# Matmuls of an identity matrix into an unread PSUM bank, in thirteen places where TensorE waits, in a hybrid decoder trunk

## The chip, the core and the metric

The kernel runs on one core of a Trainium2 chip. The metric is the device time of one execution in microseconds (us); lower is better. "TensorE" is the matmul engine, "VectorE", "ScalarE" and "GpSimd" are the elementwise engines; in the rows of the profile they are PE (PEld for its weight loads), DVE, ACT and POOL. SP is the engine that issues the weight transfers.

## What is computed

Two layers on 256 tokens of width 1024 in float32, batch 1:

```python
# layer 0
h = h + retention_mixer(rmsnorm(h), w_in, w_out)          # 4 heads, chunks of 128
h = h + swiglu(rmsnorm(h), w_gu, w_down)                  # 1024 -> 2 x 3584 -> 1024
# layer 1
h = h + conv_module(rmsnorm(h), w_pw1, w_dw, ln, w_pw2)   # depthwise width 31, LayerNorm
h = h + moe_swiglu(rmsnorm(h), w_router, w_gu, w_down)    # top 2 of 8 experts of 3584
return rmsnorm(h)
```

## The kernel before

The 256 tokens are two tiles of 128 rows. All weights stream from HBM in blocks of 1 MB (128x2048 floats): SP loads a block into one of six `raw` buffers, ScalarE copies it to `whi` (line 407, rounded to the fp32r type of TensorE), VectorE subtracts to get the rest `wlo` (line 702), and TensorE makes each product as three fp32r matmuls of 128x512 (lines 1142, 1143, 1146: high by high, high by low, low by high). Experts with at most 64 tokens use two matmuls for three (lines 1149, 1150). `whi` and `wlo` have three buffers each. Semaphores written out by hand order everything; each engine runs its own program in order, so an instruction that stands behind a waiting one waits too.

Between the weight stages TensorE has little to do and waits for the other engines:

- A norm (`turn(k)`, line 1231). ScalarE sums squares, GpSimd takes the root, VectorE writes the normalised `z` in quarters, TensorE transposes each quarter (128x128, float32) against `ident`, and ScalarE and VectorE evacuate the result to `xh` and `xl` (`xx` in the rows, lines 413 and 726). `turn(0)` opens the kernel, `turn(1)` precedes the dense SwiGLU, `turn(2)` the convolution, `turn(3)` the router.
- The LayerNorm of the convolution: sums over channels with a matrix of ones (lines 1421 and 1425), the scale spread over partitions (line 1429), and then the matmuls of `w_pw2`, which wait for `xl`.
- The router: logits (line 1443, 8 columns each), ranks (lines 1448 to 1452), the gather of the first expert's tokens with a one-hot matrix (lines 1459 and 1460, 128 columns), then `gates_first`, the first expert's gate columns.
- The end: `scatter_before(NE)` puts the last expert's output back (lines 1476 and 1477) after ScalarE and VectorE have split it.

`ident` is the first 128 columns of the constant `mats`, a transfer that ScalarE's queue issues first (line 391). A float32 matmul shows as two records in the trace, a float32 transpose and an fp32r matmul as one.

Of the kernel before, what the change touches and what calls it, by code (L numbers as in the profile page):

```python
# [17 lines left out]
SEQ, D, P = 256, 1024, 128  # L18
# [25 lines left out]
def trunk(nc, x, positions, norm_mix_g, norm_ffn_g, final_norm_g, ret_w_in, ret_w_out, conv_w_pw1,  # L44
# [6 lines left out]
    with ctx:  # L51
# [24 lines left out]
        ident, earlier, ones, iota, fold = (mats[:, i, :] for i in range(5))  # L76
# [74 lines left out]
        bank = [ctx.enter_context(nc.psum_tensor(f"bank{i}", [P, BANK], f32)) for i in range(8)]  # L151
# [109 lines left out]
        def need_before(eng, e):  # L261
            return eng.value_load(plan[0:1, 0, bass.ds(e, 1)], min_val=0, max_val=3)
# [877 lines left out]
        def _(pe):  # L1140
# [85 lines left out]
            def turn(k):  # L1226
                for t in range(TILES):
                    for c in range(DC):
                        if c % 4 == 0:
                            pe.wait_ge(z_done, 4 * k + 2 * t + c // 4 + 1)  # L1230
                        last = nc.tensor.transpose(bank[2 * t + c // 4][:, c % 4 * P:(c % 4 + 1) * P],
                                                   z[:, t, c * P:(c + 1) * P], ident)
                        if c % 4 == 3:
                            last.then_inc(zT_done, 1)

            pe.wait_ge(L["mats"], 16)
            turn(0)
            for n in range(3):
                if n == 2:
                    pe.wait_ge(small_sb, 2)  # L1240
                for half in range(2):
                    columns(2 * n + half, bank[2 * n:2 * n + 2], half, 0 if n == 0 else None)
                if n == 0:

                    pe.wait_ge(L["wdw"], 16)
                    pe.wait_ge(L["small"], 48)
                    for a in range(2):
                        nc.tensor.transpose(bank[4][:, a * 124:(a + 1) * 124], wdw[:, a, :], ident[0:124, 0:124])
                    nc.tensor.transpose(bank[4][:, 256:280], small[:, :], ident[0:24, 0:24]).then_inc(small_ps, 1)
# [6 lines left out]
            for m in range(8):  # L1256
                h = m // 2
                pe.wait_ge(acc_free, (4, 4, 10, 10, 11, 11, 12, 12)[m])
                for cc in range(2):
                    c = 2 * h + cc  # L1260
# [85 lines left out]
            def hT_turn(s):  # L1346
                pe.wait_ge(hid_done, s + 1)
                chunk_turn(0, FULL)
                chunk_turn(1, FULL).then_inc(hT_ps, 1)
# [12 lines left out]
            def step(base, s, first=False, six=0):  # L1362
# [8 lines left out]
                rows(base + 5, hTh, hTl, 2, False, False, six)  # L1371
                hT_turn(s)

            turn(1)
            pe.wait_ge(xl_done, 6)
            for half in range(2):
# [9 lines left out]
            rows(B_PW1 - 2, hTh, hTl, 0, False, False)  # L1386
            rows(B_PW1 - 1, hTh, hTl, 2, False, True)

            turn(2)
            pe.wait_ge(xl_done, 10)  # L1390

# [8 lines left out]
            for b in range(8):  # L1400
                n = b // 2
# [6 lines left out]
            for m, (c, k) in enumerate(PE_TAPS):  # L1408
                if m == PE_FIRST:
# [4 lines left out]
                                        start=k == VECTOR_TAPS.get(c, 0), stop=k == TAPS - 1)  # L1414
                last.then_inc(tap_done, 1)
            for n, c in enumerate((5, 6, 0, 1, 2, 3, 4, 7)):
                if c >= 5:
                    pe.wait_ge(y_pe, c - 4)
                else:
                    pe.wait_ge(y_done, 1)  # L1420
                last = nc.tensor.matmul(bank[0][:, 0:SEQ], ones, y[:, c, :], start=n == 0, stop=n == DC - 1)
            last.then_inc(mu_ps, 1)
            for c in range(DC):
                pe.wait_ge(sq_done, c + 1)
                last = nc.tensor.matmul(bank[1][:, 0:SEQ], ones, sq[:, c, :], start=c == 0, stop=c == DC - 1)
            last.then_inc(var_ps, 1)
            for t in range(TILES):
                pe.wait_ge(lnd_done, t + 1)
                last = nc.tensor.matmul(bank[2][:, t * P:(t + 1) * P], ones, diag[:, t, :], start=True, stop=True)
            last.then_inc(lnb_ps, 1)  # L1430
            for r in range(4):
                pe.wait_ge(vl_done, 2 * r + 2)
                rows(B_PW2 + r, xh, xl, 2 * r, r == 0, r == 3)

            turn(3)

            pe.wait_ge(res_done, 6)
            pe.wait_ge(L["wr"], 16)
            for t in range(TILES):
                pe.wait_ge(hT32_done, t + 1)  # L1440
                pe.wait_ge(hT32b_done, t + 1)
                for c in range(DC):
                    last = nc.tensor.matmul(bank[4][:, t * NE:(t + 1) * NE], hT32[:, c, t * P:(t + 1) * P], wr[:, c, :],
                                            start=c == 0, stop=c == DC - 1)
            last.then_inc(lg_ps, 1)

            pe.wait_ge(sel_done, 1)
            nc.tensor.matmul(bank[5][:, 0:NE], earlier, rk[:, 4, 0, :], start=True, stop=True)
            nc.tensor.matmul(bank[5][:, NE:2 * NE], earlier, rk[:, 4, 1, :], start=True, stop=False)
# [4 lines left out]
            def gather(e, tile):  # L1454
                for c in range(DC):
                    dst = bank[2 * tile + c // 4][:, c % 4 * P:(c % 4 + 1) * P]
                    for t in range(TILES):
                        where = onehot[:, t, tile * P:(tile + 1) * P]
                        nc.tensor.matmul(dst, zh[:, t, c * P:(c + 1) * P], where, start=t == 0, stop=False)  # L1459
                        last = nc.tensor.matmul(dst, zl[:, t, c * P:(c + 1) * P], where, start=False, stop=t == TILES - 1)  # L1460
                return last
# [18 lines left out]
            def scatter_before(e):  # L1480
                pe.wait_ge(yl_done, e + 1)
                with pe.If(need_before(pe, e) > 1):
                    pe.wait_ge(y2l_done, wide_before(pe, e))
                    scatter(2)
                with pe.Else():
                    scatter(1)
# [12 lines left out]
            def expert(e, kind, need):  # L1499
                six, done, tiles = STEPS * e, STEPS * e + STEPS, 2 if kind == WIDE else 1  # L1500
                gates_end = nothing(bank[0])
                if kind == WIDE:
                    gather(e, 1).then_inc(gather2_ps, 1)
                    scatter_before(e)
                    pe.wait_ge(xel2_done, wide_before(pe, e) + 1)
                    gates_first(1, six).then_inc(pe_done, 2)
                else:
                    gates_end.then_inc(pe_done, 2)
                    scatter_before(e)
                pe.wait_ge(hTl_done, done)  # L1510
                expert_columns(B_MOE + 2, bank[2:4], 0, kind, need, six)
                expert_columns(B_MOE + 3, bank[2:4], 1, kind, need, six)
                pe.wait_ge(res_done, 2 * e + 8)
                onehot_turn(tiles)
                for n in range(2):
                    nc.tensor.matmul(DOWN[0][n][:, :], zeros[:, 0:P], zeros[:, :], start=True, stop=False)
                if kind == WIDE:
                    pe.wait_ge(ohT_done, e + 1)
                    for n in range(2):
                        nc.tensor.matmul(DOWN[1][n][:, :], zeros[:, 0:P], zeros[:, :], start=True, stop=False)  # L1520
                expert_turn(done, kind, need)
                with pe.Fori(0, STEPS - 1) as i:
                    pe.wait_ge(silu_done, done + 1 + i)
                    columns(B_MOE + 4, bank[0:2], 0, tiles=tiles, six=six + i)
                    columns(B_MOE + 5, bank[0:2], 1, tiles=tiles, six=six + i)
                    pe.wait_ge(hTl_done, done + 1 + i)
                    expert_columns(B_MOE + 6, bank[2:4], 0, kind, need, six + i)
                    expert_columns(B_MOE + 7, bank[2:4], 1, kind, need, six + i)
                    expert_rows(B_MOE + 8, 0, False, kind, need, six + i)
                    expert_rows(B_MOE + 9, 2, False, kind, need, six + i)  # L1530
                    expert_turn(done + 1 + i, kind, need)
                pe.wait_ge(silu_done, done + STEPS)
                pe.wait_ge(onehot_done, e + 2)
                gather(e, 0).then_inc(gather_ps, 1)
                pe.wait_ge(hTl_done, done + STEPS)
                expert_rows(B_MOE + 40, 0, False, kind, need, six)
                expert_rows(B_MOE + 41, 2, True, kind, need, six)

            pe.wait_ge(zh_done, 3)
            pe.wait_ge(zl_done, 2)  # L1540
            pe.wait_ge(onehot_done, 1)
            gather(0, 0).then_inc(gather_ps, 1)
            pe.wait_ge(plan_done, 1)
            pe.wait_ge(moe_set, 5)
            with pe.Fori(0, NE) as e:
                need = need_of(pe, e)
                pe.wait_ge(xel_done, e + 1)
                gates_first(0, STEPS * e)
                with pe.If(need < 1):
                    expert(e, HALF_FULL, need)  # L1550
                with pe.Else():
                    with pe.If(need < 2):
                        expert(e, FULL, need)
                    with pe.Else():
                        expert(e, WIDE, need)
            scatter_before(NE)


# [43 lines left out]
```

## Time and profile before

| | us |
|---|---|
| median of 3 runs | 1738.55 (1737.4 to 1740.38) |
| profiled execution | 1737.84 |
| its span, first to last instruction | 1736.0 |
| TensorE busy in the span | 1621.6 (93%) |
| VectorE busy | 1254.5 (72%) |
| ScalarE busy | 1022.7 (59%) |
| mean granted TensorE clock | 0.977 of full speed |

The granted clock is the speed at which TensorE was let run: 1.00 is 2.4 GHz, 0.50 is 1.2 GHz. The ends of matmuls in the trace are modelled: their busy times overlap, and the distance from one start to the next tells the pace.

### The profile page before, as it was taken

Reading aid. Unit: us, or ns where it says so; the run is one execution under the profiler, and the core shown is the slowest. Engines: PE = TensorE matmul, PEld = TensorE weight load, DVE = VectorE, ACT = ScalarE, POOL = GpSimd, SP = SyncE. Lnnn points to the kernel's source line nnn. Section 1 sums busy time; section 2 is a strip of 40 time slices with the busy share of each in tenths; the row PEclk is TensorE's granted clock in tenths of the full one; section 3 lists DMA queues with packets and bytes.
Section 4 is the critical chain, followed back from the end, with each engine's and each line's share of the span. In section 5 each row is a group of like instructions: output and inputs, shape, how many; then the busy total and the mean of one; then the engine's idle time right before and its main releaser. Section 6 shows DMA issues by size and latency. Waiting matters only on the chain.

```text
span 1736.0 us, 20901 instructions
## 1 busy us (share of the span) xinstructions
PE 1621.6 (93%) x7353; PEld 1317.2 (76%) x7354; DVE 1254.5 (72%) x1024; ACT 1022.7 (59%) x872; POOL 120.9 (7%) x91
## 2 busy tenths in 40 slices
PE   7999989999899779989999989989999899999996
PEld 5887878888788667767778878878888777777775
DVE  5745554544569559979988878845555499999996
ACT  4344344334339437878777767744444478788784
POOL 0000000000000003003030030001000030300300
PEclk9999999999999869999999999999999999999998
DMA  9652545555442018999999979946666499999994
GB/s 354 197 194 109 182 150 194 181 189 193 166 174 74 25 43 326 393 351 368 397 366 375 368 284 369 375 145 225 211 199 212 148 354 395 378 391 395 371 395 171
DMA packets 191587, 450.75 MB, mean 260 GB/s; under 512 B 8492, under 2 KB 8892, under 8 KB 191420
## 3 DMA queue, kind: packets, MB, share of 16 engines
q1 hardware_dynamic: 189212, 445.35, 71.3%
q10 hardware_dynamic: 2336, 4.85, 0.8%
q8 instruction: 28, 0.46, 0.1%
q14 instruction: 11, 0.09, 0.0%
HBM read 449.13 MB, written 1.05 MB: 259 GB/s over the span
## 4 chain that ended last, share of the span: by engine, by line
PE 70%; DVE 11%; DMA 9%; ACT 5%; issue 4%; SPq 0%; ACTq 0%; POOL 0%; DVEq 0%; POOLq 0%
PE bank L1142 19%; PE bank L1143 19%; PE bank L1146 19%; DMA raw<-in_moe_w_down 9%; DVE wlo L702 6%; ACT whi L407 4%; PE bank L1149 3%; PE bank L1150 3%; DVE y L940 2%; PE bank L1460 1%; PE bank L1459 1%; PE bank L1341 1%; PE bank L1343 1%; DVE res L1095 1%; ACT sgate L496 1%
## 5 line engine op out<-in xcount | busy, mean ns | idle before, releaser
L702 DVE TENSOR_TENSOR wlo<-raw,whi 128x2048 fp32r<-128x2048 f32 x422 | 963.4, 2291 | 313.7 <-ACT whi L407 312.3
L407 ACT ACTIVATE whi<-raw 128x2048 fp32r<-128x2048 f32 x422 | 805.3, 1915 | 430.8 <-PE bank L1146 320.0
L1142 PE MATMUL bank<-whi,xx 128*128 128x512 f32 x1184 | 473.5, 400 | 29.9 <-DVE xx L1064 8.7
L1143 PE MATMUL bank<-wlo,xx 128*128 128x512 f32 x1184 | 466.7, 394 | 0.0
L1146 PE MATMUL bank<-whi,xx 128*128 128x512 f32 x1184 | 466.1, 394 | 0.0
L1142 PEld LDWEIGHTS bank<-whi,xx 128*128 128x128 f32 x1184 | 226.1, 191 | 80.9 <-issue 19.9
L1146 PEld LDWEIGHTS bank<-whi,xx 128*128 128x128 f32 x1184 | 225.5, 190 | 48.3
L1143 PEld LDWEIGHTS bank<-wlo,xx 128*128 128x128 f32 x1184 | 225.9, 191 | 45.1
L376 POOL TENSOR_SCALAR onehot<-mats,slot 128x64 fp32r<-128x64 f32 x64 | 110.3, 1746 | 906.8 <-PE bank L1466 906.8
L1149 PE MATMUL bank<-whi,hT 128*128 128x512 f32 x336 | 138.8, 413 | 24.0 <-DVE wlo L702 23.7
L1149 PE MATMUL bank<-whi,xx 128*128 128x512 f32 x336 | 134.0, 399 | 2.6 <-DVE wlo L702 2.4
L1150 PE MATMUL bank<-wlo,hT 128*128 128x512 f32 x336 | 132.2, 394 | 0.0
L1150 PE MATMUL bank<-wlo,xx 128*128 128x512 f32 x336 | 131.2, 390 | 0.0
L502 ACT ACTIVATE hT<-bank 128x512 fp32r<-128x512 f32 x77 | 44.6, 598 | 116.2 <-PE bank L1341 60.9
L1142 PE MATMUL bank<-whi,hT 128*128 128x512 f32 x280 | 110.0, 393 | 2.5 <-DVE hT L873 2.5
L1143 PE MATMUL bank<-wlo,hT 128*128 128x512 f32 x280 | 110.2, 393 | 0.0
L1149 PEld LDWEIGHTS bank<-whi,hT 128*128 128x128 f32 x336 | 63.1, 188 | 61.5 <-DVE wlo L702 49.6
L1146 PE MATMUL bank<-whi,hT 128*128 128x512 f32 x280 | 109.0, 389 | 0.0
L873 DVE TENSOR_TENSOR hT<-bank,hT 128x512 fp32r<-128x512 f32 x77 | 51.5, 684 | 41.8 <-ACT hT L502 41.6
L1149 PEld LDWEIGHTS bank<-whi,xx 128*128 128x128 f32 x336 | 63.0, 188 | 24.1 <-DVE wlo L702 11.8
L1150 PEld LDWEIGHTS bank<-wlo,xx 128*128 128x128 f32 x336 | 63.1, 188 | 12.3
L1150 PEld LDWEIGHTS bank<-wlo,hT 128*128 128x128 f32 x336 | 63.2, 188 | 11.6
(203 smaller groups left out, 1280.2 us busy)
## 6 DMA issues: line engine op xcount, KB each, us to landing
raw<-in_moe_w_gu SPq DMA_DIRECT2D x224, 1024.0 KB, 8.0
raw<-in_moe_w_down SPq DMA_DIRECT2D x112, 1024.0 KB, 7.9
raw<-in_ffn_w_gu SPq DMA_DIRECT2D x28, 1024.0 KB, 5.1
raw<-in_ret_w_in SPq DMA_DIRECT2D x24, 1024.0 KB, 5.8
raw<-in_ffn_w_down SPq DMA_DIRECT2D x14, 1024.0 KB, 4.9
raw<-in_conv_w_pw SPq DMA_DIRECT2D x12, 1024.0 KB, 5.1
raw<-in_ret_w_out SPq DMA_DIRECT2D x8, 1024.0 KB, 4.8
res<-in_x SPq DMA_DIRECT2D x2, 512.0 KB, 4.8
```

What stands on the lines that cost most here:

```text
L376: last = nc.gpsimd.tensor_scalar(onehot[:, n // 2, at_:at_ + HALF], iota[:, h * HALF:(h + 1) * HALF], slot[:, e + 1, n, h:h + 1], None, AL ...
L407: nc.scalar.activation(whi[base % SPLIT][:, :], raw[base % RAW][:, :], ACT.Copy).then_inc(hi_done, 1)
L496: last = nc.scalar.activation(sgate[:, t, :], bank[t][:, :], ACT.Silu)
L502: last = nc.scalar.activation(hTh[:, :, t, :], bank[2 + t][:, :].rearrange("p (c n) -> p c n", c=4), ACT.Copy)
L702: nc.vector.tensor_tensor(wlo[base % SPLIT][:, :], raw[base % RAW][:, :], whi[base % SPLIT][:, :].bitcast(f32), ALU.subtract).then_inc(lo_ ...
L873: last = nc.vector.tensor_tensor(hTl[:, :, t, :], bank[2 + t][:, :].rearrange("p (c n) -> p c n", c=4), hTh[:, :, t, :].bitcast(f32), ALU. ...
L940: ins = nc.vector.scalar_tensor_tensor(y[:, c, :], uT[:, c, k:k + SEQ], w, y[:, c, :], ALU.mult, ALU.add)
L1142: nc.tensor.matmul(dst, ah, bh, start=start, stop=False)
L1143: last = nc.tensor.matmul(dst, ah, bl, start=False, stop=stop and al is None)
L1146: return nc.tensor.matmul(dst, al, bh, start=False, stop=stop)
L1149: nc.tensor.matmul(dst, both, bh, start=start, stop=False)
L1150: return nc.tensor.matmul(dst, both, bl, start=False, stop=stop)
```

## The change

A helper `warm` issues n float32 matmuls whose two operands are both `ident`, with 128 columns, each into the same columns of a PSUM bank that nobody reads before it is written again. It is called thirteen times (236 matmuls), each time ahead of a wait. Nothing waits for these matmuls, and nothing but the constants has to be there for them to start.

```diff
+            def warm(dst, n):
+                for _ in range(n):
+                    nc.tensor.matmul(dst[:, 0:P], ident, ident, start=True, stop=True)
+
             pe.wait_ge(L["mats"], 16)
+            warm(bank[7], 24)
             turn(0)
+            warm(bank[7], 20)
             for n in range(3):
...
+            warm(bank[7], 14)
             turn(1)
             pe.wait_ge(xl_done, 6)
...
+            warm(bank[3], 14)
             turn(2)
             pe.wait_ge(xl_done, 10)
...
+                    if c == 0:
+                        warm(bank[2], 18)
                     pe.wait_ge(y_done, 1)
                 last = nc.tensor.matmul(bank[0][:, 0:SEQ], ones, y[:, c, :], start=n == 0, stop=n == DC - 1)
             last.then_inc(mu_ps, 1)
+            warm(bank[3], 10)
             for c in range(DC):
                 pe.wait_ge(sq_done, c + 1)
...
             last.then_inc(var_ps, 1)
+            warm(bank[3], 16)
             for t in range(TILES):
                 pe.wait_ge(lnd_done, t + 1)
...
             last.then_inc(lnb_ps, 1)
+            warm(bank[3], 22)
             for r in range(4):
                 pe.wait_ge(vl_done, 2 * r + 2)
                 rows(B_PW2 + r, xh, xl, 2 * r, r == 0, r == 3)
 
+            warm(bank[3], 14)
             turn(3)
...
             last.then_inc(lg_ps, 1)
 
+            warm(bank[7], 18)
             pe.wait_ge(sel_done, 1)
...
+            warm(bank[7], 26)
             pe.wait_ge(zh_done, 3)
             pe.wait_ge(zl_done, 2)
             pe.wait_ge(onehot_done, 1)
             gather(0, 0).then_inc(gather_ps, 1)
+            warm(bank[7], 18)
             pe.wait_ge(plan_done, 1)
...
+            warm(bank[0], 22)
             scatter_before(NE)
```

TensorE's program at its beginning, of the kernel before (`turn(0)` and the first matmuls on weights), and of the changed kernel:

```order
L1139 UNCONDITIONAL_BRANCH
L1231 MATMUL bank<-mats,z 128x128 x16
L1142 MATMUL bank<-whi_55,xx 128x512
L1143 MATMUL bank<-wlo_58,xx 128x512
L1146 MATMUL bank<-whi_55,xx 128x512
```

```order
L1139 UNCONDITIONAL_BRANCH
L1238 MATMUL bank<-mats 128x128 x24
L1231 MATMUL bank<-mats,z 128x128 x16
L1238 MATMUL bank<-mats 128x128 x20
L1142 MATMUL bank<-whi_55,xx 128x512
L1143 MATMUL bank<-wlo_58,xx 128x512
L1146 MATMUL bank<-whi_55,xx 128x512
```

The transposes now stand behind 24 of the helper's matmuls (L1238), and the first matmul on weights behind 20 more.

TensorE's program around the router, of the kernel before (the logits, the five rank matmuls, and the first two of 32 gather matmuls):

```order
L1231 MATMUL bank<-mats,z 128x128 x16
L1443 MATMUL bank<-wr,hT_108 128x8 x16
L1448 MATMUL bank<-rk,mats 128x8
L1449 MATMUL bank<-rk,mats 128x8
L1450 MATMUL bank<-rk,mats 128x8
L1451 MATMUL bank<-rk,mats 128x8
L1452 MATMUL bank<-rk,mats 128x8
L1459 MATMUL bank<-onehot,zh 128x128
L1460 MATMUL bank<-onehot,zl 128x128
```

The same place in the changed kernel, whose lines stand lower by 4 to 17 (L1238 is the helper's matmul):

```order
L1238 MATMUL bank<-mats 128x128 x14
L1231 MATMUL bank<-mats,z 128x128 x16
L1457 MATMUL bank<-wr,hT_108 128x8 x16
L1238 MATMUL bank<-mats 128x128 x18
L1463 MATMUL bank<-rk,mats 128x8
L1464 MATMUL bank<-rk,mats 128x8
L1465 MATMUL bank<-rk,mats 128x8
L1466 MATMUL bank<-rk,mats 128x8
L1467 MATMUL bank<-rk,mats 128x8
L1238 MATMUL bank<-mats 128x128 x26
L1474 MATMUL bank<-onehot,zh 128x128
L1475 MATMUL bank<-onehot,zl 128x128
```

Three runs of the helper's matmuls stand here between rows that followed each other directly before: 14 ahead of the transposes, 18 between logits and ranks, 26 between ranks and gather.

## Rows read from the trace of the kernel before

**Rows 1.** The page: TensorE's granted clock, tenths of full, in 40 slices.

```profile
PEclk9999999999999869999999999999999999999998
```

**Rows 2.** The page, chain that ended last: shares of the span by engine.

```profile
PE 70%; DVE 11%; DMA 9%; ACT 5%; issue 4%; SPq 0%; ACTq 0%; POOL 0%; DVEq 0%; POOLq 0%
```

**Rows 3.** Stretches: length, busy (records) of PE, PEld, DVE, ACT, POOL, granted clock, DMA share, GB/s.

```profile
222.30:229.00 6.70, 5.98 (x18) 4.74 (x19) 6.54 (x8) 4.71 (x6) 0.00 (x0) 0.50 0.24 78
471.50:474.80 3.30, 3.23 (x11) 2.58 (x12) 3.15 (x6) 2.10 (x4) 0.25 (x4) 0.50 0.06 4
573.90:577.20 3.30, 3.30 (x10) 2.45 (x8) 0.00 (x0) 0.00 (x0) 0.00 (x0) 0.50 0.00 0
587.50:594.30 6.80, 5.18 (x12) 4.11 (x13) 4.65 (x13) 6.53 (x15) 0.00 (x0) 0.50 0.01 2
618.30:648.90 30.60, 22.31 (x92) 20.71 (x91) 16.22 (x58) 11.12 (x13) 0.00 (x0) 0.50 0.02 3
150.60:153.90 3.30, 3.30 (x31) 3.25 (x30) 2.34 (x4) 2.91 (x7) 0.00 (x0) 1.00 0.00 0
```

**Rows 4.** Timeline, TensorE in the retention: start, length, then what; float32 matmuls.

```profile
154.30 0.61 PE L1276 MATMUL bank<-qT,kT 128*128 128x128 f32 x4
154.74 1.03 PE L1273 MATMUL bank<-qT,kT 128*128 128x256 f32 x4
```

**Rows 5.** Timeline and DMA issues of the start; in brackets the idle time before.

```profile
0.73 0.42 ACTq L391 DMA_DIRECT2D mats<-in_c_mats  x1
mats<-in_c_mats ACTq DMA_DIRECT2D x1, 320.0 KB, 4.5
16.65 0.77 PE L1142 MATMUL bank<-whi,xx 128*128 128x512 f32 x1 [3.25 <-DVE xx L726]
19.77 0.63 PE L1143 MATMUL bank<-wlo,xx 128*128 128x512 f32 x1
20.20 0.63 PE L1146 MATMUL bank<-whi,xx 128*128 128x512 f32 x1
```

**Rows 6.** Timeline around `turn(1)`.

```profile
218.12 0.39 PE L1143 MATMUL bank<-wlo,oTh 128*128 128x512 f32 x1
218.34 0.39 PE L1146 MATMUL bank<-whi,oTl 128*128 128x512 f32 x1
220.77 1.32 PE L1231 MATMUL bank<-mats,z 128*128 128x128 f32 x8 [2.04 <-DVE z L714]
222.99 1.97 PE L1231 MATMUL bank<-mats,z 128*128 128x128 f32 x8 [0.90 <-DVE z L714]
223.56 1.91 DVE L726 TENSOR_TENSOR xx<-bank,xx 128x512 fp32r<-128x512 f32 x3
```

**Rows 7.** Timeline, TensorE in the LayerNorm of the convolution.

```profile
572.99 4.54 PE L1421 MATMUL bank<-y,mats 128*128 128x256 f32 x12 [2.75 <-DVE y L962]
578.96 3.72 PE L1425 MATMUL bank<-sq,mats 128*128 128x256 f32 x16 [1.42 <-ACT sq L595]
585.07 0.78 PE L1429 MATMUL bank<-diag,mats 128*128 128x128 f32 x4 [2.39 <-ACT diag L598]
589.12 0.79 PE L1142 MATMUL bank<-whi,xx 128*128 128x512 f32 x1 [3.27 <-DVE xx L887]
```

**Rows 8.** Timeline, TensorE and VectorE from the router to the first expert.

```profile
619.42 6.83 PE L1443 MATMUL bank<-wr,hT 128*128 128x8 f32 x32
628.64 0.60 PE L1448 MATMUL bank<-rk,mats 128*128 128x8 f32 x2 [2.39 <-DVE rk L1009]
631.44 0.17 DVE L1019 SCALAR_TENSOR_TENSOR rk<-bank,rk 128x16 f32<-128x16 f32 x1
634.73 0.45 PE L1459 MATMUL bank<-onehot,zh 128*128 128x128 f32 x1 [3.79 <-DVE onehot L1040]
643.90 0.79 PE L1142 MATMUL bank<-whi,xx 128*128 128x512 f32 x1 [2.11 <-DVE xx L1064]
```

**Rows 9.** Timeline, TensorE at the last scatter.

```profile
1723.28 0.50 PE L1476 MATMUL bank<-yh,onehotT 128*128 128x512 f32 x1 [3.47 <-issue]
```

## Prediction

> **What bounds the kernel now.** I read the chain that ended last first: 70% of it is TensorE [rows 2]. Between the weight stages the chain passes through the other engines, and there TensorE stands idle. Then I read the granted clock, because idle time here costs twice: the clock line is 9 nearly everywhere, but dips to 8 and 6 around the conv and router [rows 1]. The windows show it: 0.50 (1.2 GHz) in the stretches at 222, 471, 574, 588 and 618 us [rows 3], each begun some 4 us after TensorE last ran without a gap: 3.7 at 222 (218.6 to 222.3) [rows 3, 6], 4.8 at 587 (582.7 to 587.5) [rows 3, 7]. What follows an idle place then runs at half pace. A 128x512 matmul starts 0.43 us after the one before at the start of the kernel [rows 5] and 0.22 to 0.23 us in the full-clock stretch [rows 6]. So a cold matmul costs 0.20 us more. At the very start the page shows no low clock, but the 0.43 us pace says that it was low.
>
> The thirteen fillers should keep the clock up over the idle places. What each costs is what it runs beyond the wait that it fills.
>
> **The price of a filler.** Float32 matmuls of this shape are in the trace: four records of 128 columns take 154.74-154.30 = 0.44 us [rows 4], two records to a matmul, so 0.22 us each at full clock. At the low clock, 32 records took 6.83 us, 0.213 each [rows 8], so 0.43 us. Thus 14 fillers take 3.1 us, 18 take 4.0, 22 take 4.8, 26 take 5.7. Idle times are counted from modelled ends (a matmul shows 0.39 us at a pace of 0.23), so fillers begin about 0.15 us earlier than the idle time does; I take that off each excess.
>
> How fast does a low clock rise again under gap-free work? From 16.65 us, the pace is still 0.43 at 20.20 [rows 5]; from 589.12 it was low until 594.3 [rows 3, 7]; from 643.90 until 648.9 [rows 3, 8]. So 4 to 5.2 us; I take 4.6.
>
> **Term by term** (minus is a gain).
>
> - Start: `mats` is issued at 0.73 and lands 4.5 us later [rows 5], at 5.2. 24 fillers begin cold: 4.6 us for 10.7 of them, then 13.3 x 0.22 = 2.9, so until 12.7. The 16 transposes, 0.11 each, end at 14.5, and 20 fillers at 18.9, where the first weight matmul started at 16.65: +2.2. Cold matmuls from 16.65 to about 20.8 are gone: 10 x 0.20 = -2.0. Net +0.2 (-0.5 to +1.3: the rise, and when `mats` lands).
> - `turn(1)`: 14 fillers from 218.6 to 221.6 instead of idling to 220.77. That 0.9 us is covered: VectorE finishes the second tile's `z` before it evacuates `xl`, at 223.56 [rows 6], and the weight matmuls wait for that. Gain: they began at the transposes' end, 224.96 [rows 6], and were cold until 229.0 [rows 3], 9.4 matmuls: -1.9 (0 to -1.9).
> - `turn(2)`: the same pattern, but of 11 records in its cold window [rows 3] 8 are transposes and 3 are weight matmuls: -0.6 (0 to -1.9).
> - LayerNorm [rows 7]: 18 fillers against 2.75 idle, +1.1; the 12 records at 0.22 take 2.6 instead of 4.54, -1.9; 10 fillers against 1.42, +0.6; 16 against 2.39, +1.0; 22 against 3.27, +1.4; then the cold matmuls from 589.12 to 594.3, 5.2/0.43 = 12 x 0.20, -2.4. Sum -0.2; the later fillers are partly covered, since ScalarE's activation stage was itself late, so I take -0.4 (-1.4 to +0.9).
> - Router: the filler ahead of `turn(3)` is covered as in `turn(1)`, and faster transposes let the logits start 0.5 earlier. Logits took 6.83 us cold [rows 8] and 3.5 at full clock; but the clock was low all through them before, and it fell 3.7 to 4.8 us after dense work had ended elsewhere, so I let it fall 2.5 us into them: 23 records warm, 9 cold, 4.4 us. -2.9 (-1.4 to -3.8).
> - Ranks: 18 fillers start cold: 4.6 us, then 7.3 x 0.22 = 1.6, together 6.2, in a wait of 2.39 [rows 8]: +3.7. Ten rank records at 0.11 instead of 0.21: -1.0.
> - Gather: VectorE needs 3.3 us from ranks to one-hot (631.44 to 634.73), TensorE idles 3.79 and now runs 5.7: +1.8. Its 32 matmuls took 643.90-2.11-634.73 = 7.1 us less a tail of 0.2, 0.21 each [rows 8]; at full clock half: -3.4. 18 fillers against 2.11: +1.7. The gate columns then lose no cold stretch from 643.90 to 648.9: 11.7 x 0.20 = -2.3.
> - Router to gates together: -2.9+3.7-1.0+1.8-3.4+1.7-2.3 = -2.4 (-4.0 to 0).
> - End: 22 fillers against 3.47 [rows 9]: +1.2; the last five scatter matmuls, cold from 1724.2 on [rows 3], -1.0: +0.2 (-0.2 to +1.2).
>
> Sum: 0.2-1.9-0.6-0.4-2.4+0.2 = -4.9 us. The profiled execution took 1737.84, which gives 1732.9; the median of the runs is 0.7 higher, so 1733.5. Where a clock dip falls differs from run to run (before spread over 3 us), and the fillers shift it in the expert loop, where there is no filler: a further 1.5 us either way. About 0.2% (3.5 us) is what a measurement of this kernel can tell from no change.
>
> The largest gain after a norm depends on whether a transpose counts as work. TensorE ran nothing but transposes from 150.60 to 153.90, 31 records, and the clock stayed at 1.00 [rows 3]. The Trainium skill ("TensorE: Matmul & The Clock Gate", Part 4) says the opposite, that the full clock does not engage for transpose mode. By that rule the clock would still drop in `turn(1)` and `turn(2)`, and the sum would be -2.4; by the row, -4.9.
>
> **Rivals.**
>
> *The fillers hold a high clock but do not raise a low one* (slower). For: 32 gather matmuls of 128 columns ran without a gap from 634.73 in a window that stayed at 0.50 to 648.9 [rows 3, 8]. Against: those are fp32r; the float32 sums over channels, also from a low clock, were followed by full clock at 577.2 [rows 3, 7], and a float32 record of 128 columns occupies TensorE 0.11 us, half of what 512 fp32r columns do. It would cost at the start: 24 x 0.43 ends at 15.5, cold transposes at 18.9, 20 x 0.43 at 27.5: +10.9. Ranks to gates: 18, 26 and 18 fillers cold are 7.7, 11.2 and 7.7 against waits of 2.4, 3.8, 2.1: +18, less the -2.9 of the logits. With the other terms as above, +23: about 1761. It decides from one place: the start alone turns the sum positive. Chance 0.08. That they do not even hold the clock (then each filler after a drop costs double, about +48, 1786): 0.03.
>
> *The expert stage swallows the router's gain* (no change). The chain holds 9% DMA [rows 2], so later experts are bound by transfers. For: time won before a stage bound by transfers is lost if these run on their own. Against: the DMA share was 0.02 from 618 to 648.9 [rows 3]; transfers wait for buffers, buffers for TensorE, so the whole stream moves forward with the gates. It leaves -4.9+2.4 = -2.5: 1736. Chance 0.19.
>
> *Transposes do not count*, the mechanism above without the row: -2.4, 1736. Chance 0.05.
>
> *Excess fillers at the upper end* (late rises at start and ranks, +1.1 and +1.2, and nothing covered in the LayerNorm, +1.3): -1.3, 1737. Chance 0.07.
>
> **Numbers.** The forecast keeps 0.58: 1733.5, its own range 1730 to 1736. The range 1729.5 to 1741 takes in the no-change rivals and leaves out the slow ones and a rare better run. Faster by over 0.2% (below 1735.1): the forecast's case, nearly all, and a little of the rivals: 0.60. Within: 0.26. Slower: 0.14, the first rival and accidents of the expert loop.
>
> **What the profile would show.** Right: clock 1.00 over 222 to 229, 471 to 475 and 574 to 594; the first weight matmul near 19 us at a pace of 0.23; logits 3.5 to 5 us; a low stretch only around logits and rank fillers, in place of 30.6 us; gather 3.6 us; gates begun near 644 minus the 2 us won before. Wrong: helper matmuls 0.43 apart for more than 6 us, a first weight matmul after 22 us, or gates that start later than they did with no faster gather. My sum fails most easily at the start and at the ranks, where fillers run cold.

## The result: no gain, 0.2% slower

The changed kernel took 1742.33 us in the median of 12 runs (1734.84 to 1745.83), the kernel before 1737.57 us in the median of its 12 (1735.81 to 1740.38). The medians differ by 4.8 us; the ratio as estimated from all runs is 1.002 with a 95% interval of 1.001 to 1.0029. The forecast was 1733.5 us. The profiled execution of the changed kernel took 1740.56 us, with a span of 1738.6.

The page of the changed kernel: the granted clock in 40 slices, the chain's shares by engine, and the queue that carries instructions (transfers, MB, share of 16 engines):

```profile
PEclk9999999999999999999999999999999999999999
PE 76%; DVE 8%; DMA 6%; ACT 5%; issue 4%; ACTq 0%; DVEq 0%; POOL 0%; SPq 0%; POOLq 0%
q8 instruction: 35, 0.57, 0.1%
```

The dip of [rows 1] is gone and the chain's DVE share fell from 11% to 8% [rows 2]. The windows of [rows 3] in the changed kernel, one stretch inside the router, and one late in the expert loop:

```profile
222.30:229.00 6.70, 5.75 (x31) 4.36 (x29) 6.70 (x8) 4.50 (x6) 0.00 (x0) 1.00 0.21 78
471.50:474.80 3.30, 3.30 (x15) 2.74 (x16) 3.30 (x4) 1.92 (x1) 0.00 (x0) 1.00 0.41 104
573.90:577.20 3.30, 3.30 (x27) 3.17 (x26) 2.89 (x9) 2.00 (x6) 0.00 (x0) 1.00 0.00 0
587.50:594.30 6.80, 6.80 (x38) 5.82 (x37) 3.45 (x9) 4.42 (x10) 0.00 (x0) 1.00 0.01 2
618.30:648.90 30.60, 30.60 (x221) 29.06 (x222) 17.61 (x56) 11.57 (x11) 0.00 (x0) 0.94 0.20 64
620.00:622.00 2.00, 2.00 (x11) 2.00 (x11) 1.75 (x9) 0.00 (x0) 0.00 (x0) 0.50 0.02 4
1483.00:1500.00 17.00, 12.12 (x42) 9.37 (x41) 8.14 (x7) 5.97 (x8) 0.00 (x0) 0.80 1.03 378
```

Five windows that stood at 0.50 stand at 1.00 or 0.94: the fillers do to the clock what they were to do. What is left is a low stretch at the first rank fillers, from 620.0 to about 623.4 (the sixth row lies in it). The last row is new. Here TensorE was busy for 12.12 of 17 us. The kernel before has this row in the same window, in which it never paused:

```profile
1483.00:1500.00 17.00, 17.00 (x97) 14.66 (x96) 13.93 (x11) 13.42 (x12) 0.00 (x0) 1.00 1.05 387
```

The timeline of the changed kernel's TensorE, from the start to the first expert, answers to [rows 5] to [rows 8]. L1238 are the fillers; a filler is two records:

```profile
5.24 7.42 PE L1238 MATMUL bank<-mats 128*128 128x128 f32 x48 [5.24 <-DMA mats<-in_c_mats]
18.63 0.47 PE L1142 MATMUL bank<-whi,xx 128*128 128x512 f32 x1
18.94 0.39 PE L1143 MATMUL bank<-wlo,xx 128*128 128x512 f32 x1
225.01 0.47 PE L1142 MATMUL bank<-whi,xx 128*128 128x512 f32 x1 [0.68 <-DVE xx L726]
566.61 1.03 PE L1431 MATMUL bank<-y,mats 128*128 128x256 f32 x4
588.62 0.47 PE L1142 MATMUL bank<-whi,xx 128*128 128x512 f32 x1
613.62 1.04 PE L1231 MATMUL bank<-mats,z 128*128 128x128 f32 x8
616.26 3.71 PE L1457 MATMUL bank<-wr,hT 128*128 128x8 f32 x32
619.83 5.89 PE L1238 MATMUL bank<-mats 128*128 128x128 f32 x36
625.56 0.29 PE L1463 MATMUL bank<-rk,mats 128*128 128x8 f32 x2
640.00 0.48 PE L1142 MATMUL bank<-whi,xx 128*128 128x512 f32 x1
```

The first weight matmul comes at 18.63 instead of 16.65 us, but the next one starts 0.31 us behind it where [rows 5] show 0.43. The logits run in 3.71 us instead of 6.83, the ranks start at 625.56 instead of 628.64, the first expert's gate columns at 640.00 instead of 643.90 [rows 8].

Each of the eight experts has one matmul of four columns of zeros (`nothing`, L1188), 5 to 8 us behind the first matmul of its pass through the loop. It is a landmark. Before, the first expert's, the sixth's and the seventh's stand at:

```profile
651.82 0.17 PE L1188 MATMUL bank<-zeros 128*128 128x4 f32 x1
1382.31 0.17 PE L1188 MATMUL bank<-zeros 128*128 128x4 f32 x1
1496.81 0.17 PE L1188 MATMUL bank<-zeros 128*128 128x4 f32 x1
```

and in the changed kernel at:

```profile
645.55 0.17 PE L1188 MATMUL bank<-zeros 128*128 128x4 f32 x1
1377.27 0.17 PE L1188 MATMUL bank<-zeros 128*128 128x4 f32 x1
1499.79 0.17 PE L1188 MATMUL bank<-zeros 128*128 128x4 f32 x1
```

So the changed kernel was 6.3 us ahead at the first expert and 5.0 at the sixth, and one expert later 3.0 behind. From the sixth to the seventh it took 122.5 us, before 114.5: **one event of 8 us is more than the whole loss**. TensorE's timeline there, in the changed kernel:

```profile
1486.26 0.40 PE L1150 MATMUL bank<-wlo,hT 128*128 128x512 f32 x1
1491.53 0.79 PE L1142 MATMUL bank<-whi,xx 128*128 128x512 f32 x1 [4.88 <-issue]
```

At 1486.26 stands the last matmul in the loop's body, at 1491.53 the first of the next pass. Between them TensorE waits 4.88 us for nothing that the profile knows ("issue"), and what follows runs at half clock for a while (0.79 us for the first matmul, a clock of 0.80 over the window). The profile names no transfer and no engine that held it back: VectorE had written the next block's `wlo` by 1484.25 and `xx` by 1485.45. What is left is the instruction stream: the loop jumps back to its head there. The waits of TensorE in the expert stage (us in total, times, longest), before:

```profile
PE bank L1476 <- issue: 8.0, 2, 4.5
PE bank L1142 <- issue: 6.2, 2, 3.5
```

and in the changed kernel:

```profile
PE bank L1142 <- issue: 11.3, 3, 4.9
PE bank L1491 <- issue: 4.5, 1, 4.5
```

The L1142 wait at the loop's head occurred twice before (764 and 1009 us) and three times now. Over the whole program the instruction queue moved 28 blocks before and 35 now (0.46 and 0.57 MB, so 16 KB each). Three to four of the seven more are the fillers' own code (943 instructions, counted in the compiled program). Within 1480 to 1500 us the queue moved four in the changed kernel, two of them as the pause begins:

```profile
q8 instruction: 4, 0.07, 1.8%
```

The kernel before has no such row in that stretch.

### The profile page after: what moved, and what is told of

Same layout as the page of the kernel before. It is cut to its first block, busy times and chain, and to the rows that moved or that the text cites. A ratio compares the mean times of both kernels' runs of the same rounds, so it can differ in the third digit from the quotient of the medians.

```text
span 1738.6 us, 21844 instructions
## 1 busy us (share of the span) xinstructions
PE 1654.9 (95%) x7825; PEld 1357.1 (78%) x7826; DVE 1254.4 (72%) x1024; ACT 1022.5 (59%) x872; POOL 121.0 (7%) x91
## 4 chain that ended last, share of the span: by engine, by line
PE 76%; DVE 8%; DMA 6%; ACT 5%; issue 4%; ACTq 0%; DVEq 0%; POOL 0%; SPq 0%; POOLq 0%
PE bank L1142 19%; PE bank L1143 19%; PE bank L1146 19%; DMA raw<-in_moe_w_down 6%; DVE wlo L702 5%; ACT whi L407 4%; PE bank L1149 4%; PE bank L1150 3%; PE bank L1238 3%; PE bank L1421 3%; PE bank L1347 1%; PE bank L1475 1%; PE bank L1474 1%; PE bank L1349 1%; DVE res L1095 1%
## 5 line engine op out<-in xcount | busy, mean ns | idle before, releaser
L1142 PE MATMUL bank<-whi,xx 128*128 128x512 f32 x1184 | 471.5, 398 | 27.8 <-issue 11.3
L1142 PEld LDWEIGHTS bank<-whi,xx 128*128 128x128 f32 x1184 | 224.5, 190 | 77.2 <-issue 19.6
L1142 PE MATMUL bank<-whi,hT 128*128 128x512 f32 x280 | 110.0, 393 | 2.5 <-DVE hT L873 2.5
```

What stands on the lines that cost most here:

```text
L1142: nc.tensor.matmul(dst, ah, bh, start=start, stop=False)
```

## The experiments

The theory: TensorE's code is loaded in blocks of 16 KB. The 214 fillers ahead of the expert loop are written out, four instructions each (two records of 128 columns with their weight loads); in the compiled program they move the loop by 855 instructions, and with the expert loop at its new place within a block, the jump back to its head has to wait for a load that it did not need before. The rivals: the 22 fillers behind the loop do it; or the fillers change the timing of the stream, wherever the code lies. All kernels but the fourth are padded with waits on a semaphore that has long been reached, put ahead of the first projections' sums (`project`). They do nothing but lie there. The edit is

```
+            def pad(n):
+                for _ in range(n):
+                    pe.wait_ge(L["mats"], 16)
...
             def project(r):
+                pad(PADS[r])
```

In the first three I took each wait for one instruction. Two share one, so the shifts were half of what their expectations say (81, 41, and 44 behind the loop); the later ones are counted in the compiled program. There the expert loop starts 13 instructions into a block before (instruction 3597, if a block holds 256, the figure of the Trainium skill, "Runtime: NRT & Kernel Launch", section "Instruction fetch mechanics"), and 100 in the changed kernel (4452). "Loop at 100" is short for that. "The kernel before" was timed again beside each group: 1737.61 us (35 runs) beside the first four, 1737.64 (21) beside the next four, 1738.46 (23) beside the last four.

**1. The changed kernel with padding** (81 instructions, loop at 181).

> The changed kernel with 169 semaphore waits (already satisfied) spread over TensorE's eight w_out blocks, so that the expert loop lies at the same offset from a 16 KB boundary of TensorE's code as in the kernel before. Theory A (the fillers win some 5 us, and the move of the expert loop in the code adds a reload of code at the start of the seventh expert): no branch longer than 1 us near 1483, code transfers about 30 to 32 in place of 35, median 1731 to 1734, 4 us below before. Theory B (the extra code stall is an accident of timing, or comes from the fillers themselves): as the changed kernel, 1740 to 1744.

1735.17 us (12 runs), ratio 0.9986 (0.9977 to 0.9995). With nothing but dead weight added, it is 7.2 us faster than the changed kernel and 2.4 faster than the kernel before, a little above the 1731 to 1734 that were expected. Its profile has only one wait at the loop's head, of 3.5 us:

```profile
PE bank L1142 <- issue: 3.5, 1, 3.5
```

**2. The kernel before with padding** (41 instructions, loop at 54).

> The kernel before without any filler, its expert loop moved by 87 satisfied semaphore waits to the offset from a 16 KB boundary that it has in the changed kernel. Theory A in its first form (the offset alone decides): the extra code stall of 7 to 8 us appears, 1743 to 1747. Theory B: 1737 to 1738, as before.

1737.95 us, ratio 0.9997 (0.9986 to 1.0008): no change. With half the shift meant, this tells only that 54 is a harmless place.

**3. The same, and 44 instructions behind the loop.**

> The same, and 88 more satisfied waits behind the expert loop, where the changed kernel has its last fillers (88 instructions), so that the code ends one 16 KB block later. Theory A in its second form (what counts is that a block follows the one in which the loop ends, and is loaded over the loop's first): the stall appears here, 1743 to 1747, and not in the run without the tail. If the offset alone decides, both show it. Theory B: neither.

1738.13 us, ratio 0.9999 (0.9988 to 1.0011). With the loop at a harmless place, code behind it costs nothing; what it does at 100 this run doesn't tell.

**4. The changed kernel without the last group.**

```
-            warm(bank[0], 22)
             scatter_before(NE)
```

> The changed kernel without the 22 fillers behind the expert loop; the loop stays where it is, the code ends one 16 KB block earlier. Theory A, second form: no stall near 1483, about 1732 to 1735. Theory A, first form, and theory B: the stall stays, 1740 to 1744.

1741.08 us (12 runs), ratio 1.0022 (1.0007 to 1.0037), and in its profile the wait is still there:

```profile
PE bank L1142 <- issue: 6.2, 2, 4.8
```

The rival of the last group falls.

**5. The kernel before at the changed kernel's place** (87 instructions, loop at 100, no filler at all).

> The kernel before without fillers, its expert loop moved by 87 instructions (174 satisfied waits, since two waits share one instruction, so the earlier shift was only 41), which is the offset from a 16 KB block that it has in the changed kernel. If the offset alone makes the code stall: a branch of over 7 us near 1489 and 1743 to 1747 us. If not (the stall then needs the fillers' 14 additional KB blocks ahead, or their timing): 1737 to 1738, as before.

1745.89 us (6 runs, 1738.29 to 1748.63), ratio 1.0043 (1.0026 to 1.0059): a loss of that size, without the change. But the profiled execution was the quickest of the six and has no long wait at 1486 us, so this run alone shows that time is lost, and not where. With six runs, of which four are long, the median also depends on how many happened to be long (experiment 11).

**6. The changed kernel at the place of the kernel before** (168 instructions, loop at 13).

> The changed kernel with all its fillers and 168 instructions of satisfied waits, which puts the expert loop at the offset that it has in the kernel before. The first shift was 81 instructions in truth and had no stall near 1483. If the stall depends on where the loop lies, none here either, and 1732 to 1736; if it came from the fillers' timing, and the first shift was luck: 1740 to 1744.

1734.61 us (12 runs), ratio 0.998 (0.997 to 0.9989). This is the change as such: 3.0 us faster. The first and the last landmark of its profile, and those of the changed kernel:

```profile
L1188 PE MATMUL bank<-zeros x8: 170/170/171, 646.6 to 1606.5; 128*128 128x4 f32 x8
```

```profile
L1188 PE MATMUL bank<-zeros x8: 170/170/170, 645.6 to 1613.6; 128*128 128x4 f32 x8
```

959.9 us from the one to the other against 968.0; the kernel before takes 959.2 (651.8 to 1611.0).

**7. Fewer fillers** (20, 17, 9, 9, 12, 6, 10, 14, 9, 10, 15, 8, 15 in place of 24, 20, 14, 14, 18, 10, 16, 22, 14, 18, 26, 18, 22), loop at 13. Each group is cut to about what the wait that it fills is long.

> Fillers trimmed to the waits that the trace of the changed kernel shows (20, 17, 9, 9, 12, 6, 10, 14, 9, 10, 15, 8, 15 in the order of the program), the expert loop at the offset of the kernel before by 213 instructions of satisfied waits. Excess cost of the fillers as I priced it: 2.2 us less at the start, about 3.5 in the LayerNorm, 3.5 between ranks and gates, 1 at the end, in part covered: 6 to 9 us below the kernel with all fillers and no stall, so 1726 to 1730. If the excess was covered anyway: 1733 to 1735.

1726.26 us (6 runs, 1721.8 to 1730.42), ratio 0.9931 (0.9914 to 0.9948): 11.4 us faster than the kernel before, 8.3 more than in the full numbers. Its first and last landmark:

```profile
L1188 PE MATMUL bank<-zeros x8: 169/170/171, 641.1 to 1600.2; 128*128 128x4 f32 x8
```

It is at the first expert 5.5 us ahead of experiment 6. Most of that was won in the LayerNorm and the matmuls behind it. From the first sum over channels to `turn(3)`, the transposes ahead of the router, it takes 42.3 us:

```profile
568.01 1.03 PE L1438 MATMUL bank<-y,mats 128*128 128x256 f32 x4
586.22 0.50 PE L1142 MATMUL bank<-whi,xx 128*128 128x512 f32 x1
610.33 1.32 PE L1231 MATMUL bank<-mats,z 128*128 128x128 f32 x8
```

The changed kernel takes 47.0 us for it (566.61 to 613.62), experiment 6 the same 47.0, the kernel before 46.4 (569.22 to 615.64). From there to the first expert it is 30.8 us here, 31.9 in experiment 6 and 36.2 before. The router in it, by its window and its logits:

```profile
618.30:648.90 30.60, 29.06 (x170) 25.70 (x171) 22.05 (x62) 14.72 (x14) 0.04 (x1) 0.89 0.28 90
613.89 6.30 PE L1464 MATMUL bank<-wr,hT 128*128 128x8 f32 x32
```

The logits ran cold here for most of their time, so that it needs 2.2 us more from `turn(3)` to the ranks than experiment 6; the fillers cut at gather and gate columns gave 3.4 back.

**8. The same fillers with the loop at 100.**

> The same trimmed fillers with the expert loop at the offset of the changed kernel (44 instructions of satisfied waits in place of 213). If the offset makes the stall: a branch of over 7 us at the start of the seventh expert, and 7 to 8 us more than the trimmed kernel at the other offset, 1733 to 1738. If not: equal to it.

1732.59 us (10 runs, 1726.69 to 1737.64), ratio 0.9967 (0.9952 to 0.9982). The place costs 6.3 us in the median here too. The profiled execution, one of the quickest, has no such wait at the seventh expert, so that its cause is the same is not shown by this run.

**9. Middle groups alone** (`turn(1)`, `turn(2)`, LayerNorm, ahead of `turn(3)`; numbers of experiment 7, loop at 13).

> The changed kernel with fillers only ahead of turn(1), turn(2), the LayerNorm's three steps, the pointwise sums behind it and turn(3), in the trimmed numbers (9, 9, 12, 6, 10, 14, 9), and 236 instructions of satisfied waits, so that the expert loop stands at the offset of the kernel before. Theory that the parts add: turn(1) 1.9 us and turn(2) 0.6 us less as in the changed kernel's profile, and the LayerNorm some 2 us less because the trimmed fillers end before what they wait for: 1733 us (1731.5 to 1735). Rival, that the trimming gained at the start and at the router alone: 1735.1 us (2.5 us under the kernel before). Rival, that the trimmed fillers no longer hold the clock: 1737.6 us.

1732.17 us (6 runs), ratio 0.9953 (0.9935 to 0.9972): 6.3 us faster, below the expected 1733 but within its range. Its timeline from the logits on, where it has no filler:

```profile
616.04 3.91 PE L1464 MATMUL bank<-wr,hT 128*128 128x8 f32 x32
622.35 0.60 PE L1470 MATMUL bank<-rk,mats 128*128 128x8 f32 x2 [2.39 <-DVE rk L1009]
637.61 0.79 PE L1142 MATMUL bank<-whi,xx 128*128 128x512 f32 x1 [2.11 <-DVE xx L1064]
```

The logits take 3.91 us instead of 6.83 [rows 8]: that gain belongs to the group ahead of `turn(3)`. And the ranks start 2.4 us behind the logits' end, as before, and not 5.6 as in the changed kernel, whose 18 fillers stand in their way. The stretch from the first sum over channels to `turn(3)` is 42.4 us here (570.13 to 612.49), 4.1 less than before: that is the largest part of the 6.3.

**10. Router groups alone** (10 ahead of the ranks, 15 ahead of the gather, 8 behind it; loop at 13).

> The changed kernel with fillers only between the router's logits and the expert loop, in the trimmed numbers (10 ahead of the ranks, 15 ahead of the gather, 8 behind it), and 124 instructions of satisfied waits (the offset of the kernel before). Theory that the parts add: the trimmed kernel's 11.4 us less what the middle (4.5 us) and the start and end (2 us) give: 5 us, so 1732.6 us (1731 to 1734.5). Rival, that these fillers only work where turn(3) before them was already at the full clock: the logits stay at 1.2 GHz (2.9 us less of gain): 1735.5 us. Rival, that the expert loop takes the gain back in its first expert's weights: 1737.6 us.

1736.96 us (12 runs), ratio 0.9988 (0.9976 to 1.0): 1.5 us, not 5, and slower than the first rival's 1735.5 too. That rival's mechanism is in the profile: the groups meet a clock that is already down.

```profile
620.39 6.83 PE L1464 MATMUL bank<-wr,hT 128*128 128x8 f32 x32
627.08 4.61 PE L1238 MATMUL bank<-mats 128*128 128x128 f32 x20
631.49 0.43 PE L1470 MATMUL bank<-rk,mats 128*128 128x8 f32 x2
```

Ten fillers take 4.61 us in place of an idle 2.39. From `turn(3)` to the first expert this profile is still 2.7 us shorter than before (33.5 against 36.2), but in the loop, where its second wait at the head is 3.3 us long, it gives as much back: in this profile the second rival has a part too.

**11. Experiment 5 again.**

> The same kernel as in the fifth experiment (the kernel before, no fillers, with the expert loop at the changed kernel's offset), for a profile of an execution at its median. Theory of the reload by offset: 1745.9 us again (1744 to 1747.5), and the profile shows a stall of TensorE of 7 to 8 us in the loop's jump near 1485 to 1500 us, with more code transfers around it than the kernel before has. Rival, that its time came from elsewhere: the time is repeated but no stall stands in a profile whose span is over 1742 us.

1740.88 us (12 runs), ratio 1.0017 (1.0001 to 1.0032), less than the 1744 to 1747.5 expected. The runs fall into two clusters: eight lie between 1735.41 and 1741.69, four between 1746.26 and 1751.27. The profiled execution, with a span of 1749.5, is of the upper cluster and shows the event in a kernel without a filler:

```profile
1501.11 0.79 PE L1142 MATMUL bank<-whi,xx 128*128 128x512 f32 x1 [4.85 <-issue]
```

```profile
L1188 PE MATMUL bank<-zeros x8: 170/170/170, 652.9 to 1623.3; 128*128 128x4 f32 x8
```

970.4 us between the landmarks, 8.0 of them more than before from the sixth to the seventh (1386.79 to 1509.32). Experiments 5 and 11 are one program, and of their 18 runs eight are over 1745 us. At this place the event happens in some executions and not in others.

**12. The kernel before with 110 instructions** (loop at 123).

> The kernel before with 110 instructions of satisfied waits, so that the expert loop starts 23 instructions further into its block than in the kernel with 87. Theory that what counts is a block boundary that the narrow expert's code ends just behind (some 5 instructions in the kernel with 87): here the boundary lies 28 instructions into it, and the result tells how wide the bad place is; I take it as still bad: 1745 us (1742 to 1748). Rival, that the bad place is narrow: 1738 us (1736.5 to 1739.5).

1746.29 us (6 runs, 1745.17 to 1749.12), ratio 1.0043 (1.0027 to 1.0059), with the wait in its profile:

```profile
1498.70 0.79 PE L1142 MATMUL bank<-whi,xx 128*128 128x512 f32 x1 [4.74 <-issue]
```

Here all six runs are long: the bad place is not narrow.

In all fourteen profiles taken, the way from the sixth landmark to the seventh is either 122.5 us (the changed kernel, 4, 11 and 12, each with a wait of 4.7 to 4.9 us marked "issue" at the loop's head) or 114.4 to 115.0 (the ten others, without it).

| loop starts at | kernels | median against a like kernel |
|---|---|---|
| 12 or 13, 54, 181 | before, 1, 2, 3, 6, 7, 9, 10 | no event in any profile |
| 100 | changed, 4, 5, 8, 11 | +7.7 us (changed against 6), +6.5 (4 against 6, which still has the last group), +8.3 (5), +6.3 (8 against 7), +2.4 (11); no event in the profiles of 5 and 8 |
| 123 | 12 | +7.8 us |

The instruction queue separates the two kinds as well. Behind the sixth landmark each of the ten quiet profiles has a transfer within 24 us, and the four with the event have none until the jump; there they have four. One program shows both: the first line is experiment 5 from 1382 to 1480 us (experiment 11 has no such line from 1387 to 1490), the second is experiment 11 around the jump, from 1495 to 1510 us:

```profile
q8 instruction: 1, 0.02, 0.1%
q8 instruction: 4, 0.07, 2.5%
```

This points to a block of code that is loaded during the sixth expert in the quiet executions, and only at the jump in the others.

The Trainium skill ("Runtime: NRT & Kernel Launch", section "Instruction fetch mechanics") says that code comes in blocks of 16 KiB (256 instructions), that prefetch is sequential, and that a taken branch whose target is not resident has to wait for a fetch. The trace agrees: blocks of 16 KB, and 4.7 to 4.9 us of idle TensorE at the jump while such blocks are moved. The page calls the cost of a block's edge mostly hidden; in a loop as long as this one it is so for most jumps and not for all.

## Why the prediction was wrong

**The step that failed** is the one on the expert loop. The text said: "the fillers shift it in the expert loop, where there is no filler: a further 1.5 us either way". That term was for where the clock dips fall. The text took the loop for work that moves forward as a whole, and gave code loading no term. The loop did move forward, by 5.0 us up to the sixth expert; then one jump cost 8.0. The chance of 0.14 for slower named "accidents of the expert loop" without a mechanism. The trace of before held a sign of one: the waits marked "issue" at the loop's head, 6.2 us in all, were there to be read, and so were 28 loads on the instruction queue. An edit that writes 214 matmuls out in front of such a loop moves it to another place. With the loop at the old place (experiment 6) the same fillers gave 1734.61 us, inside the forecast's own 1730 to 1736, though a gain of 3.0 us and not of 4.9: the rest of the sum was right in kind and too large.

**Term by term**, from the landmarks of the profiled executions:

| term | forecast | measured |
|---|---|---|
| start | +0.2 | 0.0 (the transposes of `wdw` behind the first projections at 29.6 in both) |
| `turn(1)` | -1.9 | -1.9 (first gate transposes after it at 450.4, before 452.3) |
| `turn(2)` | -0.6 | -0.7 (first sum of the LayerNorm at 566.6, before 569.2) |
| LayerNorm to `turn(3)` | -0.4 | +0.6 (`turn(3)` 613.62, before 615.64) |
| router to the first expert | -2.4 | -4.3 (645.55, before 651.82) |
| expert loop up to the sixth | 0 | +1.3 (-5.0 left) |
| jump after the sixth | none | +8.0 |
| last expert, end | +0.2 | -0.4 |

The sum is +2.6, the difference of the spans. Single profiles scatter: the seven profiles of kernels without fillers ahead of it (before, 2, 3, 5, 10, 11, 12) reach the first sum of the LayerNorm anywhere from 566.6 to 571.0, so the first three rows are no proof of their terms; that the cold stretches there are gone is shown by the windows. From that sum to `turn(3)` six of the seven take 46.4 or 46.5 us (experiment 3: 44.7) and the four with full groups 47.0. From `turn(3)` to the first expert six take 36.2 (experiment 10, which has fillers there: 33.5) and those with full groups 31.9 (experiment 4: 33.6). So these two rows stand: the LayerNorm's groups cost more than they gave, and the router's gave 1.9 us more than forecast. The end's cold stretch, for which the text names [rows 3], is in no row there; a window shows it:

```profile
1724.20:1736.00 11.80, 2.17 (x6) 1.17 (x4) 5.68 (x10) 2.30 (x4) 1.11 (x2) 0.50 0.24 89
```

Up to the first expert the sum is -6.3 against a forecast of -5.1. In the router the logits were warm throughout, so that `turn(3)` and logits gave -4.3 (they end at 619.97 against 626.25, 6.3 us sooner, 2.0 of it won earlier) where the sum had -2.9. The rank fillers cost 3.2 (ranks at 625.56, 3.1 ahead instead of 6.3) where it had 3.7. From ranks to first expert the forecast was -3.2 (-1.0+1.8-3.4+1.7-2.3) and the trace says -3.2 (19.99 us against 23.18).

**The rivals.** That fillers do not raise a low clock is refuted: the clock stood at 0.50 from 620.0 under the rank fillers and at 1.00 from 624.0, and TensorE had run nothing but fillers in between. That they do not hold a high one is refuted by the windows. *The expert stage swallows the router's gain*: no, 5.0 of 6.3 us were still there at the sixth expert, and experiments 6 and 7 keep it to the end. *Transposes do not count*: its forecast, that the clock would still drop in `turn(1)` and `turn(2)`, is refuted, since the windows stand at 1.00 through 16 transposes. The Trainium skill ("TensorE: Matmul & The Clock Gate", Part 4) says that transpose mode does not engage the full clock, and that stays undecided. From the last filler to the first weight matmul only 3.3 us pass at `turn(1)` (221.71 to 225.01). The row on which the prediction rested is no longer: the transposes in it ran from 149.94 to 153.43, 3.5 us, and matmuls of the retention fill its end. In the kernel before the clock had fallen only 3.7 us after the last dense work ahead of `turn(1)` [rows 3] [rows 6]. *Excess fillers*: their direction was right and their weight too small. Trimming won 8.3 us; of the 7.7 us between the spans of the profiles of 6 and 7, 5.5 lie ahead of the first expert (641.1 against 646.6; 4.7 of them between the first sum of the LayerNorm and `turn(3)`), 0.8 in the loop and 1.4 at the end. I priced them by the wait that each overran and let the overrun stand. That a smaller number holds the clock nearly as well (0.89 in the router's window of experiment 7) was not asked.

**What stays open.** Why a loop start at 100 or 123 brings the reload and 13, 54 and 181 do not, and why at 100 it comes in some executions only, wasn't settled. Every kernel here has other waits marked "issue" (4.5 or 4.6 us ahead of a scatter between 1139 and 1154 us in all fourteen profiles), which a full rule would have to account for. Nor is each of them a cost of code: after the first expert eleven profiles have such a wait of about 3.5 us, and in those of 4, 8 and 11 TensorE stands there nearly as long for VectorE, as in experiment 4:

```profile
761.25 0.58 PE L1142 MATMUL bank<-whi,xx 128*128 128x512 f32 x1 [3.42 <-DVE wlo L702]
```

The 3.6 us by which the middle groups and the router groups together (6.3 and 1.5 us) fall short of the 11.4 of experiment 7 don't come from the LayerNorm or the router. Against the kernel before, from the first sum of the LayerNorm to the first expert the profiles are shorter by 6.9 us in experiment 9, by 2.7 in experiment 10 and by 9.5 in experiment 7. What is left lies at the start, at the end, in the loop or in the scatter of the runs, and wasn't split.

## What to carry to other kernels

Before you price an edit that adds or removes many instructions ahead of a long loop, look in the trace of before for waits marked "issue" at the loop's head and for the instruction queue's transfers. If they are there, give the shift a term of its own (here 0 or 8 us in one execution), and separate it in the measurement: the same kernel, padded with waits that are long met, at the old place. Then size a filler by the wait that it fills, in the time that it takes at the clock it meets: where the clock is already down it costs double (ten took 4.61 us in experiment 10, and eighteen warm ones would take 4.0).

## What the runs showed of the hardware

- The place of a loop in its code blocks is worth 2.4 to 8.3 us of 1738 in the median. Two kernels with the same work differ by it: 1742.33 and 1734.61 us.
- One program can have the wait in one execution and not in the next: it stands in the profile of experiment 11 (1751.27 us) and not in that of experiment 5 (1738.29 us).
- A pause of 4.9 us cost 8.0: what follows it runs at the lower clock level, 1.2 GHz (0.50 from 1491.5 to 1497.2). Behind 1491.53 thirteen matmuls start 0.43 us apart instead of 0.23, until 1497.2: 2.6 us. The last 0.5 us I did not trace.
- Nine fillers ahead of `turn(3)` kept the clock up through 16 transposes with a pause of 0.88 us and through the logits (3.91 us) in the profile of experiment 9; the same nine did not in that of experiment 7 (6.30 us). Fourteen did in the changed kernel's (3.71 us).
